# Order of work at the seams between head rounds: mLSTM rows turned after the next round's first quarter, v split before q, weights split behind late columns

## What is computed

```python
xn = rms_norm(h, norm_mix_w)
proj = einsum('bsd,de->bse', xn, w_in)      # q, k, v of both mixers, mLSTM i, f, o, branch gates
oa = rms_norm(diff_attention(qa, ka, va, lam, cos, sin), da_subln_w) * (1 - lambda_init)   # 8 heads
ob = sigmoid(ml_o) * rms_norm(mlstm_chunkwise(qm, km, vm, i_pre, f_pre), ml_norm_w)        # 8 heads
merged = g[:, :, 0] * (oa @ w_proj_a) + g[:, :, 1] * (ob @ w_proj_b)
h = h + merged @ w_out
h = h + (relu(rms_norm(h) @ w_ff1) ** 2) @ w_ff2
return rms_norm(h, final_norm_w)
```

## Time and profile before

| | |
|---|---|
| median of 3 runs | 1956.83 us |
| profiled execution, its own time | 1959.85 us |
| span of its instructions | 1957.6 us |
| PE, weight loads, DVE, ACT, POOL busy | 97%, 81%, 61%, 49%, 19% |
| mean granted clock of TensorE | 0.997 |

### The profile page before, as it was taken

One profiled execution on the slowest core, in us unless ns is written; L12 is line 12 of the kernel. 1 busy time (PEld: TensorE's weight loads), 2 busy tenths in 40 slices (PEclk: granted clock), 3 DMA queues, 4 the chain that ended last, 5 costly groups with the idle time before them and its releaser, 6 DMA issues. The chain is left out here.

```text
span 1957.6 us, 25826 instructions
## 1 busy us (share of the span) xinstructions
PE 1906.0 (97%) x9314; PEld 1592.5 (81%) x9314; DVE 1188.0 (61%) x1538; ACT 958.3 (49%) x1618; POOL 365.8 (19%) x203
## 2 busy tenths in 40 slices
PE   6999999999999999999999999999999999999998
PEld 5788888888888888878888888878887888888886
DVE  6755666666665757543422122488777777789774
ACT  4355565656564655544434223226485665433341
POOL 1221212112121121212223444440000000121002
PEclk9999999999999999999999999999999999999999
DMA  4251514242423333252244434457576686564412
GB/s 168 89 172 55 178 55 157 74 150 86 148 88 123 107 101 134 72 173 67 81 158 144 156 119 159 174 192 269 201 273 235 211 295 223 187 235 146 155 65 86
DMA packets 91872, 291.77 MB, mean 149 GB/s; under 512 B 10872, under 2 KB 11640, under 8 KB 80784
## 3 DMA queue, kind: packets, MB, share of 16 engines
q1 hardware_dynamic: 89488, 282.31, 41.9%
q10 hardware_dynamic: 2304, 8.39, 1.1%
HBM read 203.56 MB, written 87.10 MB: 148 GB/s over the span
## 5 line engine op out<-in xcount | busy, mean ns | idle before, releaser
L708 PE MATMUL gp<-r1h,w_hi 128*128 128x512 f32 x1152 | 454.6, 395 | 2.2 <-POOL w_lo L1910 2.2
L710 PE MATMUL gp<-r1h,w_lo 128*128 128x512 f32 x1152 | 450.1, 391 | 0.0
L709 PE MATMUL gp<-r1l,w_hi 128*128 128x512 f32 x1152 | 449.5, 390 | 0.0
L1910 POOL TENSOR_TENSOR w_lo<-w_raw,w_hi 128x1024 fp32r<-128x1024 f32 x87 | 218.1, 2507 | 857.3 <-ACT w_hi L1036 857.3
L710 PEld LDWEIGHTS gp<-r1h,w_lo 128*128 128x128 f32 x1152 | 216.6, 188 | 46.4
L708 PEld LDWEIGHTS gp<-r1h,w_hi 128*128 128x128 f32 x1152 | 216.7, 188 | 45.4 <-POOL w_lo L1910 2.6
L709 PEld LDWEIGHTS gp<-r1l,w_hi 128*128 128x128 f32 x1152 | 216.9, 188 | 41.8
L956 PE MATMUL scores<-xh,qh 128*128 128x512 f32 x512 | 200.3, 391 | 3.2 <-ACT res L1309 2.3
L958 PE MATMUL scores<-xl,qh 128*128 128x512 f32 x512 | 199.2, 389 | 0.0
L960 PE MATMUL scores<-xh,ql 128*128 128x512 f32 x512 | 199.2, 389 | 0.0
L1158 ACT ACTIVATE pr<-scores,nb 128x256 f32<-128x256 f32 (+7 forms) x128 | 93.8, 738 | 117.8 <-DVE nb L1544 116.2
(11 more groups left out here) (327 smaller groups left out, 3698.2 us busy)
## 6 DMA issues: line engine op xcount, KB each, us to landing
xraw<-xo_d SPq DMA_DIRECT2D x54, 1024.0 KB, 5.4
w_raw<-in_in_blocks SPq DMA_DIRECT2D x64, 512.0 KB, 3.7
proj_d<-ev SPq DMA_DIRECT2D x128, 256.0 KB, 2.0
rq<-in_ff_quarters SPq DMA_DIRECT2D x32, 1024.0 KB, 8.0
xo_d<-res SPq DMA_DIRECT2D x78, 256.0 KB, 3.3
xo_d<-ring SPq DMA_DIRECT2D x60, 256.0 KB, 3.0
pr<-proj_d SPq DMA_DIRECT2D x16, 512.0 KB, 4.6
gt<-proj_d SPq DMA_DIRECT2D x32, 256.0 KB, 3.5
```

The source lines that it names most:

```text
L708: pe.matmul(gp[half][:], wh[slot][:, k, :], mh[:, k, t], start=(k == 0), stop=False)
L709: pe.matmul(gp[half][:], wh[slot][:, k, :], ml[:, k, t], start=False, stop=False)
L710: mm = pe.matmul(gp[half][:], wl[slot][:, k, :], mh[:, k, t], start=False, stop=(k == KT - 1))
L1910: pool.tensor_tensor(wl[slot][:], raw[slot][:], wh[slot][:].bitcast(F32), ALU.subtract).then_inc(w_split, 1)
```

## The change

It has three parts. The turning of the mLSTM rows leaves slot 15 and is issued in the next round, behind the first quarter of its first unit; the gate round issues its units in quarters for that, and turns its own head's rows behind slot 15. In slot 0 ACT makes v's high parts before q's, and DVE v's low parts before q's. In the slots from 9 on ACT splits a weight block behind the high part of the late columns instead of before `attend`; that concerns slots 10 and 12 of the head rounds.

```diff
@@ tensor
-                if s == 15:
-                    pe.wait_ge(hm_ready, h + 1)
-                    pe.wait_ge(ot_out, 2 * h + 2)
-                    for i, bank in enumerate((tr, ob)):
-                        for j in range(4):
-                            mm = pe.transpose(bank[:, j * P:(j + 1) * P], nd[:, 4 * i + j, 0:DV], ident[:])
-                        mm.then_inc(hm_tr, 1)
-
-            def head_round(h, att):
+
+            def ml_turned(h):
+
+                pe.wait_ge(hm_ready, h + 1)
+                pe.wait_ge(ot_out, 2 * h + 2)
+                for i, bank in enumerate((tr, ob)):
+                    for j in range(4):
+                        mm = pe.transpose(bank[:, j * P:(j + 1) * P], nd[:, 4 * i + j, 0:DV], ident[:])
+                    mm.then_inc(hm_tr, 1)
+
+            def head_round(h, att, turn=None):
                 for s in range(SLOTS):
                     for part in range(8 * HB):
                         if QUARTER_AT[part] == s:
                             head_unit(h, part // 4, part % 4)
+                            if part == 0 and turn is not None:
+                                ml_turned(turn)
                     attend(att, s)
 
             head_round(1, 0)
             with pe.Fori(2, NH) as h:
-                head_round(h, h - 1)
+                head_round(h, h - 1, h - 2)
             for s in range(SLOTS):
                 for k in GATE_UNITS_AT[s]:
-                    unit(N_GATE + k // 2, k // 2 % 2, k % 2, r1h, r1l)
+                    for part in range(4):
+                        unit(N_GATE + k // 2, k // 2 % 2, k % 2, r1h, r1l, quarter=part)
+                        if k == 0 and part == 0:
+                            ml_turned(NH - 2)
                 attend(NH - 1, s)
+            ml_turned(NH - 1)
@@ scalar
-            def attend(h, s, evac_units):
+            def attend(h, s, evac_units, splits=None):
...
                             evac_units()
-                    v_part(0)
-                    v_part(1)
+                            v_part(0)
+                            v_part(1)
...
                 i = s - 5
+                if 4 <= i < TT:
+                    high(i, True)
+                if splits:
+                    splits()
                 if 0 <= i < TT:
-                    if i >= 4:
-                        high(i, True)
                     act.wait_ge(pv_done, TT * h + i + 1)
...
                 for s in range(SLOTS):
-                    for k in STARTS_AT[s]:
-                        if k % 2 == 0:
-                            units_of_round(h, k)
+                    def splits():
+                        for k in STARTS_AT[s]:
+                            if k % 2 == 0:
+                                units_of_round(h, k)
+
+                    if s < 9:
+                        splits()
                     for k in ENDS_AT[s][:-1]:
                         evac(h * HB + k // 2, k % 2)
...
-                    attend(att, s, evac_units)
+                    attend(att, s, evac_units, splits if s >= 9 else None)
@@ vector
-                    low_parts(1, qraw, qs)
                     for i in range(2):
                         dve.wait_ge(v_hi, 2 * h + i + 1)
                         src = (tr, ob)[i][:].rearrange("p (t n) -> p t n", t=4)
                         dve.tensor_tensor(vs[:, 4 * i:4 * i + 4, DV:2 * DV], src, vs[:, 4 * i:4 * i + 4, 0:DV].bitcast(F32),
                                           ALU.subtract).then_inc(v_lo, 1)
+                    low_parts(1, qraw, qs)
```

## The result

The changed kernel takes 1970.26 us in the median of 4 runs (1968.68 to 1972.0), against 1957.16 (1956.29 to 1957.89, 4 runs) before: ratio 1.0065, 95% interval 1.0053 to 1.0077. It is 13.1 us slower; 11.7 over the earlier median was forecast, and 1968.5 as the time. The profiled execution took 1969.36 us.

A forecast was written before the change was run, and what follows sets the result against it. TensorE, busy 97% of the span, bounds the kernel, with DVE and ACT setting when slot 3's scores start. Scores +19.1, slot 10 −5.1 and gate round −2.4 sum to +11.6 us, hence 1968.5 us; range 1956.5 to 1979.

The forecast's parts named there:

- The first quarter waits for k=10's evacuation: At a round's start, the quarter waits for gp0 until about 422.48: a stall of 1.8 us in place of 1.0.
- k=2 waits too: In the transition between rounds, TensorE waits for k=0's evacuation at 436.39, and k=2 starts at 436.5.
- The collision: POOL's weight split delays DVE's second q low part to 446.0; slot 3's scores start 3.2 us later, six times: +19.1.
- The sentence of the Trainium skill: Only two-port VectorE modes block against GpSimd; q's low parts would pass, and the sum be +0.3 instead of +11.6.
- Slot 10: With ath's late part before the weight split, TensorE's wait for atl goes: −0.73 us, seven rounds, −5.1.
- Slot 13 was covered: POOL's qpad ends at 410.65, but slot 13 starts at 410.86 for cst: covered by 0.2 us, nothing taken.
- The whole round: Period of the rounds: 106.8 us instead of 104.4.
- The gate round: The product behind 2.22 us of idle starts 0.7 us earlier, its half clock goes (1.7 us): together −2.4.
- The clock rival: Half clock behind the new 1.9 us stall before the scores in each of six rounds: 10 us more, 1979; chance 0.17.
- The clock term: At the gate round, the half clock behind the stall goes with the stall at 0.9: 1.7 us saved.
- the sum: Whole kernel: +19.1 − 5.1 − 2.4 = +11.6 us.
- the 2.06 forecast: In the transition between rounds, DVE gets the turned rows 2.06 us later, and everything behind moves with it.

The follow-up runs named there:

- part 1 alone: Kernel before, with only the turning of the mLSTM rows moved behind the next round's first quarter: 1973.17 us, ratio 1.0074.
- the early evacuation: Changed kernel, with ACT evacuating k=10 before attend in slot 13 instead of after: 1958.38 us, ratio 0.9999 to the kernel before.
- the run with POOL held: Changed kernel, with POOL's split of slot 2 waiting until the q low parts are done: 1958.47 us, ratio 1.0005 to the kernel before.
- part 3 alone: Kernel before, with only ACT's weight split moved behind the late columns' high part in slots 10 and 12: 1950.43 us, ratio 0.996.
- their two causes repaired: Changed kernel, with k=10 evacuated before attend in slot 13 and POOL's slot 2 split held until q's low parts are done: 1944.85 us, ratio 0.994.
- the early split without part 1: Kernel before, with the late-column change, k=10 evacuated early and the next round's first weight split in slot 13; turning stays in slot 15: 1947.1 us.
- the early split with part 1: Changed kernel, but q before v as originally, k=10 evacuated early and the next round's first weight split in slot 13: 1941.15 us, ratio 0.9921.
- part 2 alone: Kernel before, with only v's high and low parts put ahead of q's: 1961.87 us, ratio 1.002.

## Why the prediction was right, step by step

- **The first quarter waits for k=10's evacuation.** Right in place and size. It was put at 422.48, which with the 3.92 us is 426.40; it starts at 426.37. The turning came at 427.86 (427.8 forecast), DVE's `osig` at 428.59 (428.46). The runs with part 1 alone and with the early evacuation show it from both sides.
- **k=2 waits too.** Forecast at 440.42, started at 440.47.
- **The collision.** POOL was to ask at 445.84 and did at 445.95, inside the first q low part; the second took 3.28 us. The scores were forecast at 449.97 and start at 450.24; 0.1 us of the rest is the step from the last v low part to the first q part, 0.71 us where I had taken 0.61. Holding POOL undoes it.
- **The sentence of the Trainium skill** on two-port modes (Advanced Engine Details and Errata, VectorE Performance Modes), taken as the whole list of what blocks, would have made this kernel some 11 us faster than it is (12 is what the run with POOL held shows). The prediction took it so; the sentence names these modes and doesn't say that nothing else blocks. The operation of 1.22 us that becomes 3.28 decides against that reading. What the Trainium skill says in SBUF — State Buffer, under SBUF: two separate sides, that an operation with two SBUF inputs takes the shared ports as a lock against a GpSimd operation that reads SBUF, agrees with these traces; v's low parts, which read PSUM, keep their 0.68 us beside POOL. The small `nb`, with one input, was held as well (1.10 us instead of 0.17 in the run with POOL held).
- **Slot 10** was sized 0.73 us a round; alone it is 0.79. Slot 13 was covered, as said: its wait for `cst` is the same seven times and 2.7 us. The whole round, forecast at 106.8 us, is 106.6 to 106.8 in five of six.
- **The gate round.** Its stall is 0.72 us of idle where I had 0.9 in all, and no half clock follows in the profile:

```profile
879.81 0.50 PE L708 MATMUL gp<-r1h,w_hi 128*128 128x512 f32 x1 [0.72 <-POOL w_lo L1924]
```

- **The clock rival** (a half clock behind the scores' stall in each of six rounds) was right in kind, too high in number. The changed kernel's profile has it once:

```profile
665.30:668.50 3.20, 3.20 (x9) 2.42 (x9) 1.57 (x5) 0.81 (x4) 0.00 (x0) 0.50 0.96 245
```

It made that round 108.4 us long, 1.6 over the others.
- **The clock term** of the sum is what was mis-sized. The forecast took 1.7 us off for the half clock at the gate round and put none behind the scores. The first went, but the profile has one in the other place, so in the clock nothing was won: the four executions of the changed kernel have mean clocks of 0.998, 0.997, 0.999 and 0.997 (1969.36, 1971.16, 1968.68 and 1972.0 us), 0.9978 in the mean, and the 43 of before 0.9977. Without its clock term the sum is 13.3. The stretch that the change touches, from the first head's first scores to the first feed-forward matmul, is 12.9 us longer in the profile (1200.7 against 1187.8 us, a half clock in each). So the waits came out within 0.4 us of the sum, and the clock gave back nothing where 1.7 was expected; most of the 1.5 us between 11.6 and the measured 13.1 is this term.
- **Part 1 alone** cost 2 us more than worked out. The rounds in its profile are 106.5 us long, 2.15 over before, near the 2.06 forecast, and the same stretch is 13.7 us longer, against 13.2. Its five executions have a mean clock of 0.9968 where the session's of before have 0.9975, which by the figures under part 3 is some 0.9 us more (an estimate). Some 0.7 us stays open.
- **The spans.** The two profiled spans differ by 9.7 us (1957.6 to 1967.3) where the medians differ by 13.1, because the profiled execution of before took 1959.85 us, 2.7 over its median of 1957.16, and that of the changed kernel 1969.36, 0.9 under its own. The profile of before had a second half clock, in the feed-forward part, that the one after has not:

```profile
1921.40:1924.60 3.20, 3.20 (x9) 2.62 (x10) 0.54 (x2) 0.00 (x0) 0.35 (x1) 0.50 0.02 5
```

## What to carry to other kernels

Before a step is put behind other work to hide its wait, ask what that other work waits for: here the quarter that was to cover 1.0 us waited 1.8 us for its bank, and the engine that frees the bank had been idle earlier. When operations of DVE change their order, look at what POOL does in the same stretch: an order that leaves the sum of DVE's work alone can turn a harmless neighbour into 2 us, six times. Take a change of several parts apart: one part here was worth 7.5 us and hidden under two that cost 19, and with their two causes repaired the whole change gained 12.6.

## What the hardware showed that was not expected

- A half clock does not follow every long stall. Behind the stall for `w_lo` at the gate round (2.2 us of idle) it came in the profiles of before, of part 1 alone and of the early split without part 1, and not in those of part 3 alone and of the early split with part 1. Behind the scores' stall (1.75 to 1.8 us of idle) it came once in six with the change, never in six with part 2 alone, twice in six with the early evacuation. Behind the stall of 1.60 us at the first quarter it never came. A stall of this length is a risk of 1.6 us, not a certain price, and how great a risk differs between kernels with the same stall: nine of 11 executions with the early evacuation have a mean clock of 0.997, and nine of 11 with part 2 alone have 0.998 or 0.999. Why is open.
- POOL and DVE take turns, and it runs both ways: POOL's split took 3.07 us because it was held behind DVE's first part, DVE's second 3.28 behind POOL, and then POOL's copy of 128x32 elements 1.23 us, at 0.23 us otherwise, behind DVE's end.
